# Expert chunks cut by half depth, and one looped copy of the code for further tokens

## The reference

```python
def hier_moe(h, grp_w, grp_b, rtr_w, rtr_b, w_gate, w_up, w_down):
    ...
    expert_id = g_idx[:, None] * EXPERTS_PER_GROUP + top_i          # two of 16 experts for each token
    combine = jnp.sum(jax.nn.one_hot(expert_id, N_EXPERTS, dtype=jnp.float32) * top_w[..., None], axis=1)
    hidden = jax.nn.silu(jnp.einsum('nd,edf->nef', x, w_gate)) * jnp.einsum('nd,edf->nef', x, w_up)
    y = jnp.einsum('nef,efd->nd', hidden * combine[:, :, None].astype(hidden.dtype), w_down)
```

## Time and profile before

| | us |
|---|---|
| median of 3 runs | 1363.14 |
| lowest, highest | 1362.69, 1367.03 |
| the profiled execution | 1359.36 |
| its span, first to last instruction | 1357.6 |
| TensorE matmuls busy in it | 1254.6 |
| VectorE, ScalarE, GpSimd busy | 517.5, 298.7, 131.5 |

### The profile page before, as it was taken

How to read it: one execution, slowest core, us unless ns; L and a number is a source line. 1 busy time by engine, 2 the same in 40 slices (tenths; PEclk the granted TensorE clock), 3 DMA queues, 4 the chain that set the end, 5 groups by cost and what they waited for, 6 DMA issues and landing times. The chain is left out here.

```text
span 1357.6 us, 14639 instructions
## 1 busy us (share of the span) xinstructions
PE 1254.6 (92%) x5786; PEld 704.8 (52%) x5786; DVE 517.5 (38%) x1016; ACT 298.7 (22%) x712; POOL 131.5 (10%) x139
## 2 busy tenths in 40 slices
PE   4999989998999899798999999999999979999897
PEld 2543346445544435244767766776776445454332
DVE  1275666143100002445544645645565551000035
ACT  2123245032111110105121222211232231111112
POOL 0069900000000001001101000000000000000010
PEclk9999999999999999899999999999999999999999
DMA  9859996465999995631232321332234759999994
GB/s 380 331 183 366 372 422 244 168 259 191 383 401 427 425 426 219 283 125 39 102 124 70 140 78 70 132 120 82 78 140 195 316 202 361 411 420 426 425 423 197
DMA packets 35388, 344.67 MB, mean 254 GB/s; under 512 B 3920, under 2 KB 9296, under 8 KB 16080
## 3 DMA queue, kind: packets, MB, share of 16 engines
q1 hardware_dynamic: 23184, 315.36, 57.5%
q0 software_dynamic: 4608, 16.78, 3.1%
q10 hardware_dynamic: 7488, 11.01, 2.2%
HBM read 324.53 MB, written 18.61 MB: 253 GB/s over the span
## 5 line engine op out<-in xcount | busy, mean ns | idle before, releaser
L803 PE MATMUL PS<-ring,hT 128*64 128x512 f32 x736 | 234.8, 616 | 18.8 <-issue 13.8
L610 PE MATMUL PS<-ring,hT 128*128 128x512 f32 x432 | 190.3, 594 | 0.2 <-ACT hT L1150 0.2
L803 PE MATMUL PS<-area,hT 128*64 128x512 f32 x272 | 127.8, 627 | 12.4 <-issue 12.4
L803 PEld LDWEIGHTS PS<-ring,hT 128*64 128x64 f32 x736 | 78.7, 142 | 104.6 <-issue 104.6
L610 PEld LDWEIGHTS PS<-ring,hT 128*128 128x128 f32 x432 | 81.1, 190 | 98.6 <-issue 97.8
L815 PE MATMUL PS<-ring,area 128*64 128x512 f32 x400 | 113.3, 595 | 2.9 <-issue 2.0
L995 PE MATMUL PS<-ring 128*128 128x256 f32 x480 | 108.7, 379 | 1.2 <-ACT ring L1433 1.2
L995 PEld LDWEIGHTS PS<-ring 128*128 128x128 f32 x480 | 91.1, 190 | 13.9 <-issue 1.6
L1973 DVE TENSOR_TENSOR area<-area,PS 128x512 f32<-128x512 f32 x16 | 11.0, 687 | 225.8 <-PE PS L803 225.8
L976 PE MATMUL PS<-ring,area 128*128 128x512 f32 x192 | 83.8, 593 | 3.8 <-ACT area L1521 3.8
L995 PE MATMUL PS<-ring,hT 128*128 128x256 f32 x360 | 82.6, 379 | 0.0
(11 more groups left out here) (302 smaller groups left out, 1506.0 us busy)
## 6 DMA issues: line engine op xcount, KB each, us to landing
ring<-moe_w_down SPq DMA_DIRECT2D x25, 2048.0 KB, 19.3
ring<-mod_w SPq DMA_DIRECT2D x24, 2048.0 KB, 11.6
ring<-moe_w_up SPq DMA_DIRECT2D x24, 2048.0 KB, 15.0
ring<-moe_w_gate SPq DMA_DIRECT2D x22, 2048.0 KB, 15.0
ring<-in_w SPq DMA_DIRECT2D x21, 2048.0 KB, 8.2
area<-moe_w_up SPq DMA_DIRECT2D x8, 2048.0 KB, 13.2
area<-moe_w_gate SPq DMA_DIRECT2D x8, 2048.0 KB, 14.9
ring<-out_w SPq DMA_DIRECT2D x7, 2048.0 KB, 8.1
```

What stands on the lines that cost most here:

```text
L610: mm = pe.matmul(out, lhs(k), rhs(k), start=n == 0, stop=n == KD - 1)
L803: mm = pe.matmul(PS[64 * e:64 * e + 64, j, :], g[:, k, 64 * e:64 * e + 64], W[e][k], start=k == 0, stop=k == KD - 1)
```

## The change

Two things are changed together. First, a chunk of expert weights no longer holds one expert's whole matrix: it holds half the depth (half of the rows that are summed over) of both experts of the pair. The products run through the first half for both experts, then through the second half, and wait for each chunk where they first need it; the first half of the gate product waits for the first half of the gathered tokens only. Each half of a product releases its slot by itself, so the counts of `expert_free` double. Second, on TensorE alone, the first unit's straight copy and the loop behind it become one copy of `unit` in two nested loops, 2 groups of `OVG` = 5 passes, each group and each pass with an If on n. ScalarE and VectorE keep their two copies.

The diff, cut to its core:

```diff
+OVG = 5
@@ released
-                eng.wait_ge(expert_free[c % 6 // 2], PAIRS * l + c // 6 + 1)
+                eng.wait_ge(expert_free[c % 6 // 2], 2 * (PAIRS * l + c // 6) + c % 2 + 1)
@@ TensorE
-                def up(j, g, W):
-
-                    for k in range(KD):
-                        for e in range(2):
-                            mm = pe.matmul(PS[64 * e:64 * e + 64, j, :], g[:, k, 64 * e:64 * e + 64],
-                                           W[e][k], start=k == 0, stop=k == KD - 1)
-                    return mm
+                def up(j, p, half_mm):
+
+                    W = [[], []]
+                    for half in range(2):
+                        w = here(6 * p + 2 * j + half)
+                        if j == 0:
+                            pe.wait_ge(gath_copied, 2 * (base + p) + half + 1)
+                        for k in range(4):
+                            for e in range(2):
+                                mm = pe.matmul(PS[64 * e:64 * e + 64, j, :], gT[:, 4 * half + k, 64 * e:64 * e + 64],
+                                               w[e][k], start=half == 0 and k == 0, stop=half == 1 and k == 3)
+                        if half == 0:
+                            mm.then_inc(half_mm, 1)
+                        W = [W[e] + w[e] for e in range(2)]
+                    return mm, W
...
+                def down(p):
+
+                    W = [[], []]
+                    for part in range(2):
+                        w = here(6 * p + 4 + part)
+                        for half in range(2):
+                            for k in range(2):
+                                for e in range(2):
+                                    mm = pe.matmul(PS[64 * e:64 * e + 64, 5 + half, :], hidT[:, 2 * part + k, 64 * e:64 * e + 64],
+                                                   w[e][k][:, half * 512:half * 512 + 512],
+                                                   start=part == 0 and k == 0, stop=part == 1 and k == 1)
+                            if part == 1:
+                                mm.then_inc(down_mm, 1)
+                        if part == 0:
+                            mm.then_inc(down_half, 1)
+                        W = [W[e] + w[e] for e in range(2)]
+                    return W
...
@@ TensorE, the Else behind the down product
-                        unit(p, a, b, c, e, W)
-                        with pe.If(n > CAP + OVC):
-                            with pe.Fori(1, OVS) as u:
-                                with pe.If(n > u * OVC + CAP):
-                                    unit(p, u * da + a, u * db + b, u * dc + c, u + e, W)
-                                with pe.Else():
-                                    pe.wait_ge(ov_pe, u * da + a)
-                                    pe.sem_inc(ov_pe, da)
-                                pe.nop()
-                        with pe.Else():
-                            pe.wait_ge(ov_pe, a + da)
-                            pe.sem_inc(ov_pe, da * (OVS - 1))
-                        pe.nop()
+                        with pe.Fori(0, OVS // OVG) as v:
+                            with pe.If(n > v * (OVG * OVC) + CAP):
+                                with pe.Fori(0, OVG) as u:
+                                    with pe.If(n > v * (OVG * OVC) + u * OVC + CAP):
+                                        unit(p, v * (OVG * da) + u * da + a, v * (OVG * db) + u * db + b,
+                                             v * (OVG * dc) + u * dc + c, v * OVG + u + e, W)
+                                    with pe.Else():
+                                        pe.wait_ge(ov_pe, v * (OVG * da) + u * da + a)
+                                        pe.sem_inc(ov_pe, da)
+                                    pe.nop()
+                            with pe.Else():
+                                pe.wait_ge(ov_pe, v * (OVG * da) + a)
+                                pe.sem_inc(ov_pe, OVG * da)
+                            pe.nop()
@@ ScalarE
-                    act.wait_ge(egate_mm, g + 1)
-                    act.activation(sgate, PS[:, 0, :], ACT.Silu).then_inc(silu_done, 1)
                     with act.If(n < CAP + 1):
+                        act.wait_ge(gate_half, g + 1)
                         act.sem_inc(expert_free[0], 1)
+                        act.wait_ge(egate_mm, g + 1)
+                        act.sem_inc(expert_free[0], 1)
+                        act.activation(sgate, PS[:, 0, :], ACT.Silu).then_inc(silu_done, 1)
+                        act.wait_ge(up_half, g + 1)
+                        act.sem_inc(expert_free[1], 1)
                         act.wait_ge(eup_mm, g + 1)
                         act.sem_inc(expert_free[1], 1)
+                    with act.Else():
+                        act.wait_ge(egate_mm, g + 1)
+                        act.activation(sgate, PS[:, 0, :], ACT.Silu).then_inc(silu_done, 1)
@@ VectorE
                     with dve.Else():
+                        dve.wait_ge(down_half, g + 1)
+                        dve.sem_inc(expert_free[2], 1)
                         dve.wait_ge(down_mm, 2 * g + 2)
                         dve.sem_inc(expert_free[2], 1)
...
```

More of the change, by code:

```diff
@@ L408, in backbone_kernel @@
         expert_free = [sem("gate_free"), sem("up_free"), sem("down_free")]
+        gate_half, up_half, down_half = map(sem, ("gate_half", "up_half", "down_half"))
         ov_pe, ov_act, ov_dve, ov_key, ov_stored = map(sem, ("ov_pe", "ov_act", "ov_dve", "ov_key", "ov_stored"))
@@ L531, in _ @@
                     fill(i, expert(l, c))
-            sp.wait_ge(expert_free[2], 2 * PAIRS - 1)
+            sp.wait_ge(expert_free[2], 4 * PAIRS - 2)
             sp.dma_start(fg, fgain).then_inc(fg_loaded, 16)
@@ L769, in here @@
                     if PLACE[i] == APART:
-                        return [v.rearrange("p a b -> p (a b)")[:, 512 * k:512 * k + 512] for v in (gate_row, G) for k in range(4)]
-                    w = wslot(i)
-                    return [w[:, k, :] for k in range(4 if c % 6 >= 4 else KD)]
+                        return [[v.rearrange("p a b -> p (a b)")[:, 512 * k:512 * k + 512] for k in range(4)] for v in (gate_row, G)]
+                    w, n = wslot(i), 2 if c % 6 >= 4 else 4
+                    return [[w[:, n * e + k, :] for k in range(n)] for e in range(2)]
                 def token_rows(p):
@@ L894, in pair @@
                     d = 2 * l + p - DIRECT
-                    pe.wait_ge(gath_copied, 2 * g + 2)
                     if p == 2:
                         pe.wait_ge(gate_copied, 4 * s + 4)
[L898 to L901, removed]
+                    mm, W = up(0, p, gate_half)
+                    mm.then_inc(egate_mm, 1)
+                    mm, w = up(1, p, up_half)
+                    mm.then_inc(eup_mm, 1)
+                    W += w
                     next_tokens(p, 0)
@@ L919, in pair @@
                         gate_rows(s, (0, 1, 2, 3), [1])
-                    W += [here(6 * p + 4), here(6 * p + 5)]
                     pe.wait_ge(hidT_copied, g + 1)
@@ L923, in pair @@
                     need(pe, ov_act, b)
-                    for half in range(2):
-                        down(half, W[4:6]).then_inc(down_mm, 1)
+                    W += down(p)
                     if direct:
@@ L1308, in unit @@
                     with act.If(n < bound):
-                        act.sem_inc(expert_free[0], 1)
+                        act.sem_inc(expert_free[0], 2)
                         act.wait_ge(ov_pe, a + 3)
-                        act.sem_inc(expert_free[1], 1)
+                        act.sem_inc(expert_free[1], 2)
                     act.wait_ge(ov_pe, a + 4)
@@ L1395, in pair @@
                                 act.nop()
-                        act.sem_inc(expert_free[2], 1)
+                        act.sem_inc(expert_free[2], 2)
                     with act.Else():
@@ L1968, in pair @@
                     if p == 1:
-                        dve.wait_ge(expert_free[0], base + 1)
+                        dve.wait_ge(expert_free[0], 2 * base + 1)
                         gate_diag(s)
@@ L2301, in slots, with pair_halves @@
         return w.reshape(n * r, P, rows // P * columns)
+    def pair_halves(w, k, columns):
+        w = w.reshape(PAIRS, 2, 2, k, P, columns).transpose(0, 2, 4, 1, 3, 5)
+        return w.reshape(2 * PAIRS, P, 2 * k * columns)
     for n, rows, columns in (("mod_w", 256, 2048), ("in_w", D, 512), ("out_w", 512, D)):
@@ L2305 @@
     for n, rows, columns in (("moe_w_gate", D, FF), ("moe_w_up", D, FF), ("moe_w_down", FF, D)):
-        args.append([given(f"{n}{l}", slots(a[f"{n}{l}"].reshape(-1, columns), rows, columns)) for l in range(2)])
+        args.append([given(f"{n}{l}", pair_halves(a[f"{n}{l}"], rows // (2 * P), columns)) for l in range(2)])
     args += [made("y_out", (NT, D)), made("new_k", (KH, P, HD)), made("new_v", (KH, P, HD)),
```

2 lines of the change are left out of this document (1 added, 1 removed).

## The result

| | before | after |
|---|---|---|
| median of 6 runs, us | 1362.91 | 1352.27 |
| lowest, highest | 1358.75, 1367.03 | 1346.85, 1352.83 |
| the profiled execution, us | 1359.36 | 1349.07 |
| its span | 1357.6 | 1347.3 |

The ratio of after to before is 0.9913, with a 95% interval of 0.9894 to 0.9932: the kernel became faster by 0.9%, 10.6 us. The forecast was 1433 us, slower.

What follows compares the result with a forecast made beforehand. The prediction took TensorE's idle time at long branches as the bound, DMA second. Loops +35.6 and +26.4, passes +10, waits -2.2 gave +69.8 us on 1363.14: 1433 us, range 1385 to 1470.

Steps and rivals of the forecast that it cites:

- What bounds the kernel: TensorE's idle time, mostly long branches behind expert pairs (26.3 us in 13 waits); then DMA, weights leading by 2.5 us.
- (4), the loops: Two pairs with further tokens: 10 branches across a unit each, at 3.34 or 6.1 us; +35.6 and +26.4 us.
- (5), the passes' instructions: Counters, sums, waits and increments in the loops of the two pairs with further tokens: 5 us a pair, +10 us.
- (3), the shorter skips: Behind 14 pairs without further tokens, skipping one copy costs as much as two: nothing; 2.0 us per cheap skip.
- If a skip or two is served: Side case: one or two skips find their target loaded while loops are dear; forecast moves down 2 to 5 us.
- (1), the chunks: Half-depth chunks cut TensorE's waits ahead of gate, up and down products: -2.2 us; earlier free slots worth nothing.
- The loops run from code that is kept: Rival: code that has run stays loaded, so the loops' branches cost about 0.1 us; 1361 us, chance 0.08.
- The shorter skip is served: Rival: skips over one copy find their target loaded, 14 gaps vanish, weights limit the gain; 1343 us, chance 0.10.

Runs made afterwards that it cites:

- The kernels without the code: Changed kernel and kernel before, each without TensorE's If and unit code in the 14 pairs that need none: 1336.99 and 1353.21 us.
- The chunks alone: Changed kernel with TensorE's old two copies of the unit instead of the nested loops: 1350.46 us, 0.9910 of before.
- the halves together: Changed kernel with both slots of a product released together at its end, as before: 1357.35 us in group 2, 1356.56 us in group 3.
- The aligned kernel: Changed kernel with never-run matmuls ahead of 11 pairs' Ifs, so all 14 skips begin at the same place of a block: 1348.29 us.

## Why the prediction was wrong

**What bounds the kernel** was right in the experts of both layers: TensorE's idle time, the branches as its largest part, and the weights close behind. The kernels without the code showed both.

**(4), the loops: wrong, and this is the step that gave the sign.** The prediction counted the branches rightly, 10 crossings in each pair. Their price was taken from the row nearest by distance, L945 in the earlier trace rows, 6119 and 3338 ns. That row is a jump to code that had never run. In a loop the code on both sides of the branch has just run, and the crossings measured 0.21 us each (none over 0.24). The nearest row was chosen by how far the branch goes and should have been chosen by whether its target had been there; the short branch of 0.07 to 0.09 us in the earlier trace rows was the nearer end. The 62 us of this term were 0. (Rows of before could not show it, and the prediction said so; the bound of 0.08 us stood in the text, and the case that goes with it was given a chance of 0.08.)

**(5), the passes' instructions: right in size, wrong in the sum.** They were taken at 5 us a pair and measured 6.7 us with their branches. In the first pair 6.1 us stood there before as one long branch, and in the second pair all of it is covered. The +10 us of the sum are +0.4 us, since the sum added them to dear branches that didn't come.

**(3), the shorter skips: nearly right.** The gap of "about 2.3 us" that the prediction named at first was 2.0 us in the mean, as its own 26.3/13 says. One of 14 was served and returned its 2.1 us; of the 13 others none was served, though four are shorter for another reason (below). "If a skip or two is served" was foreseen, with that price. The chunks alone have no served skip and are as fast as the change, so its 2.1 us are read from the gap and can't be told from noise in the times.

**(1), the chunks: mis-sized.** The -2.2 us for waits came as said: the gap of 0.69 us ahead of each layer's first gate product and the 0.8 us for the down chunk are gone. "Slots come free earlier ... that is worth nothing now. It hides behind the long branch" failed. The earlier transfers shorten the long branch itself, where the DMA engines aren't yet full, because the code packet starts 1.0 us after the branch and not 3.0: the gaps ahead of pair 1 go from 1.39 and 1.19 us to none, those ahead of pair 2 from 2.44 and 2.42 to 1.49 and 1.74. These four are -4.2 us where the term had 0, and taking the early release away cost 5.0 us. The prediction had the row that says it: the earlier trace rows tie the price of a branch to the DMA load around it, and (1) moves that load.

**The sum as it should have been**, from the two profiles: waits -2.2, four branches -4.2, one served skip -2.1, other gaps +1.5 (0.4 of it the loops) = -7.0. The gate products add -2.7 us: before as after, some of those that follow a gap run at a lower clock, 8.4 to 8.8 us in place of 6.9. Two windows of the changed kernel show one product of each kind (length, busy PE, PEld, DVE, ACT, POOL, clock, DMA share, GB/s):

```profile
438.70:445.60 6.90, 6.90 (x33) 2.80 (x35) 0.00 (x0) 0.00 (x0) 0.00 (x0) 1.00 1.01 423
468.10:476.80 8.70, 8.57 (x32) 3.34 (x34) 0.37 (x1) 0.00 (x0) 0.00 (x0) 0.80 1.02 426
```

A mean granted clock of 0.80 over the product means that a part of it ran at the lower of the two levels, 1.2 GHz. Which pairs it hits changes from one profile of the same kernel to the next (7 products before, 5, 4 and 5 in the three profiles of the changed kernel, 4 and 8 in the two with the halves together), so that this term is not the change's for certain. Together -9.7 of the -10.3 us between the spans.

**The rivals.** "The loops run from code that is kept" had the mechanism and gave 1361 us; it was 9 us too high for the same missing term in (1). "The shorter skip is served" gave 1343 us for the case that all 14 are served. The aligned kernel is that case: 0.9894 of 1363 is 1349 us. The direction was right, and so in part was the limit, weights that come late; the gain that it left, 20 us, was too large. It had no term for the code behind the skip's target, which came late as well.

## What to carry to other kernels

Price a branch by whether its target has run lately and still fits in what is kept, not by its distance: on TensorE a loop over some 1350 instructions crossed in 0.2 us, while a skip over 420 that had never run cost 3.3 to 7.2 us. A jump to new code is a small DMA transfer that starts behind larger ones (2.7 to 4.7 us later here, against 0.9 to 1.0 with idle DMA engines), so whatever is done to the order or the start of transfers changes its price. And before a cost that hides others is removed, price what is behind it: half of what the branches held up went at once to waits for weights, and the change was worth 14 us once that was the limit.

## What the runs showed of the hardware that was not expected

- TensorE keeps at least 1350 and fewer than 2370 instructions that have run; taken crossings within them take 0.19 to 0.32 us in both directions, also while the DMA engines are full.
- A jump to code not loaded takes 3.3 to 3.8 us with idle DMA engines: some 1.0 us until its code packet starts, 0.9 to 1.3 us for the packet, 1.4 us until the branch ends. With weights in the engines the first part grows to 2.7 to 4.7 us and the branch to 5.1 to 7.2 us.
- A skip over about 420 instructions costs 0.7 to 3.8 us if it begins at the right place of a block, and up to 7.2 us elsewhere, with the same code. TensorE's queue of matmuls then covers all of it, so that its own gap is zero up to about 3.8 us (0.34 us in the one case at 3.78).
- Removing 20.7 us of gaps by alignment returned no more than 1 to 3 us. 6.0 us came back as stops in the middle of gate products, each behind a code packet. Why some weights land later there than in the kernel without the code stays open.
